# Two weight-block sums per group made by adding transfers that GpSimd issues, in a two-layer hybrid encoder trunk

## The reference, cut to what matters

```python
def swiglu(u, w_in, w_out):
    gate, up = jnp.split(u @ w_in, 2, axis=-1)
    return (jax.nn.silu(gate) * up) @ w_out

x = x + MACARON_WEIGHT * rms_norm(
    swiglu(rms_norm(x, ffn1_pre_norm[l]), ffn1_w_in[l], ffn1_w_out[l]), ffn1_post_norm[l])
```

## Time and profile before

| what | value |
|---|---|
| median of 3 runs | 2174.72 us (2173.4 to 2174.93) |
| the profiled execution's own time | 2174.53 us |
| its span in the profile | 2172.7 us |
| TensorE busy | 2141.5 us, 99% |
| VectorE busy | 1440.2 us, 66% |
| ScalarE busy | 1046.9 us, 48% |
| GpSimd busy | 75.3 us, 3% |
| mean load of the DMA engines' memory side | 101 GB/s |

### The profile page before, as it was taken

The page is one execution under the profiler, slowest core; times in us unless marked ns, Lnnn a source line. Parts: engine busy times, 40 slices in busy tenths (PEclk is TensorE's granted clock), DMA queues, the critical chain, the costliest instruction groups (busy, mean ns, idle before and its releaser), DMA issues. The chain is left out here.

```text
span 2172.7 us, 34540 instructions
## 1 busy us (share of the span) xinstructions
PE 2141.5 (99%) x14060; PEld 1926.6 (89%) x14060; DVE 1440.2 (66%) x1877; ACT 1046.9 (48%) x1802; POOL 75.3 (3%) x104
## 2 busy tenths in 40 slices
PE   8899999999999999999999999999999999999998
PEld 7899988888888899998899998887888889999987
DVE  7999735595536598873388885356944456988633
ACT  5444424655533465552375454256555436554422
POOL 0000000011000100000000000010000001000000
PEclk9999999999999999999999999999999999999999
DMA  5233332332123323323233323323322243223332
GB/s 217 91 104 108 97 97 78 127 85 79 59 78 103 140 95 110 110 86 109 85 108 117 107 88 107 97 88 117 85 69 69 78 141 117 92 107 101 105 97 78
DMA packets 80302, 218.71 MB, mean 101 GB/s; under 512 B 19216, under 2 KB 29968, under 8 KB 79376
## 3 DMA queue, kind: packets, MB, share of 16 engines
q1 hardware_dynamic: 78128, 203.92, 28.9%
q0 software_dynamic: 2016, 12.58, 1.6%
HBM read 208.87 MB, written 7.60 MB: 100 GB/s over the span
## 5 line engine op out<-in xcount | busy, mean ns | idle before, releaser
L1662 DVE TENSOR_TENSOR wlo<-raw,whi 128x1024 fp32r<-128x1024 f32 (+1 forms) x215 | 261.3, 1216 | 371.4 <-ACT whi L1137 368.7
L1137 ACT ACTIVATE whi<-raw 128x1024 fp32r<-128x1024 f32 (+1 forms) x212 | 221.1, 1043 | 422.0 <-PE ps L748 275.4
L808 PE MATMUL ps<-chi,lor 128*128 128x256 f32 x1280 | 363.0, 284 | 0.0
L670 PE MATMUL ps<-uhi,whi 128*128 128x512 f32 (+1 forms) x864 | 310.2, 359 | 4.8 <-ACT sk L1410 2.6
L672 PE MATMUL ps<-uhi,wlo 128*128 128x512 f32 (+1 forms) x864 | 302.6, 350 | 0.0
L671 PE MATMUL ps<-ulo,whi 128*128 128x512 f32 (+1 forms) x864 | 302.5, 350 | 0.0
L806 PE MATMUL ps<-chi,hir 128*128 128x256 f32 x1024 | 292.1, 285 | 6.3 <-DVE lor L1789 5.7
L807 PE MATMUL ps<-clo,hir 128*128 128x256 f32 x1024 | 290.7, 284 | 0.0
L746 PE MATMUL ps<-whi,hhi 128*128 128x512 f32 x704 | 274.5, 390 | 0.0
L747 PE MATMUL ps<-wlo,hhi 128*128 128x512 f32 x704 | 273.9, 389 | 0.0
L748 PE MATMUL ps<-whi,hlo 128*128 128x512 f32 x704 | 273.9, 389 | 0.0
(11 more groups left out here) (303 smaller groups left out, 3921.7 us busy)
## 6 DMA issues: line engine op xcount, KB each, us to landing
raw<-in_wstream_dram SPq DMA_DIRECT2D x207, 512.0 KB, 3.5
lof<-in_swstream_dram SPq DMA_DIRECT2D x80, 512.0 KB, 3.6
r<-in_swstream_dram SPq DMA_DIRECT2D x60, 512.0 KB, 4.6
ulof<-in_swstream_dram SPq DMA_DIRECT2D x20, 512.0 KB, 6.0
x_home<-x POOLq DMA_DIRECT2D x4, 1024.0 KB, 4.3
x<-x_home POOLq DMA_DIRECT2D x2, 2048.0 KB, 9.3
gain<-in_gp_dram POOLq DMA_DIRECT2D x6, 512.0 KB, 5.6
raw<-in_wstream_dram SPq DMA_DIRECT2D x10, 256.0 KB, 3.6
```

The source lines that it names most:

```text
L670: pe.matmul(o, lh, bhi, start=first, stop=False, skip_group_check=True)
L808: last = pe.matmul(o, ll, bhi, start=False, stop=True, skip_group_check=True)
L1137: act.activation(whi[:, s, 0:cols], raw[:, s % RAWS, 0:cols], ACT.Copy).then_inc(hi_done.h, 1)
L1662: dve.tensor_tensor(wlo[:, s, 0:cols], raw[:, s % RAWS, 0:cols], whi[:, s, 0:cols].bitcast(f32), ALU.subtract) \
```

## The change

The two sums `sum_3` and `sum_11` leave DVE. In their place two transfers make each sum in its slot: SP loads one block there as an ordinary transfer, and when that has landed, GpSimd issues a transfer of the other block with an addition (`accum_op=ALU.add`) into the same slot. For `sum_3` the first is W_22 (so W_22 is loaded twice, once for its own use and once for this) and the added one W_12; for `sum_11` the first is W_12 and the added one W_11 (loaded twice too). `sum_22` and `sum_4` stay on DVE. The buffer `r12` is gone, and its 4 KB become a ninth slot of the low parts; so W_11 and W_21 load behind the product nine earlier instead of eight. In the head the W_12 load of the first group moves ahead of the x tiles. GpSimd's adds for an FFN stand between its other work at the FFN's boundaries. Some waits at the end of an FFN follow the new slot numbers.

```diff
-LO_SLOTS, HI_SLOTS = 8, 5
+LO_SLOTS, HI_SLOTS = 9, 5
...
-        LO_AT, HI_AT = (136, 140, 152, 156, 148, 180, 168, 172), (56, 160, 176, 164)
+        LO_AT, HI_AT = (136, 140, 152, 156, 148, 180, 48, 168, 172), (56, 160, 176, 164)
...
-        r12 = at("r12", [P, 4, 256], 48 * kb)
...
             sp.dma_start(raw[:, 0, :], wstream[2]).then_inc(raw_ready[2].h, 16)
+            sp.dma_start(whole(0, 1, Q_C), weights(0, 0, 1, W_12)).then_inc(first11.h, 16)
             for i in range(TT):
                 sp.dma_start(x[:, i, :], xin[i]).then_inc(x_in[i].h, 16)
...
-                load_part(L, f, 1, W_12, r12[:, :, :])
+                    sp.dma_start(whole(f, 1, Q_C), weights(L, f, 1, W_12)).then_inc(first11.h, 16)
                 sp.wait_ge(gemm_done.h, gemm_done.at(L, unit))
                 load_part(L, f, 1, W_22, r22[1])
                 sp.wait_ge(split_done.h, split_done.at(L, c + 3))
                 load_part(L, f, 1, W_11, whole(f, 1, Q_A))
+                sp.wait_ge(split_done.h, split_done.at(L, c + 4))
+                sp.dma_start(whole(f, 1, Q_D), weights(L, f, 1, W_22)).then_inc(first3.h, 16)
...
-                    sp.wait_ge(*of_group(sum11, L, f, g - 1))
-                    sp.wait_ge(*of_group(sum3, L, f, g - 1))
-                    load_part(L, f, g, W_12, r12[:, :, :])
...
                     load_part(L, f, g, W_22, r22[g % 2])
+                    if g > 2:
+                        sp.wait_ge(*of_unit(unit_done, L, f, unit_no(g, Q_D) - LO_SLOTS))
+                    sp.wait_ge(*of_unit(unit_lo, L, f, unit_no(g - 1, Q_D)))
+                    sp.dma_start(whole(f, g, Q_D), weights(L, f, g, W_22)).then_inc(first3.h, 16)
                     sp.wait_ge(*of_unit(unit_done, L, f, unit_no(g, Q_A2) - LO_SLOTS))
                     load_part(L, f, g, W_21, whole(f, g, Q_A2))
+                    sp.wait_ge(*of_unit(unit_done, L, f, unit_no(g, Q_C) - LO_SLOTS))
+                    sp.dma_start(whole(f, g, Q_C), weights(L, f, g, W_12)).then_inc(first11.h, 16)
...
-                dve.tensor_tensor(whole(f, g, Q_D), r12[:, :, :], r22[g % 2], ALU.add).then_inc(sum3.h, 1)
...
-                dve.tensor_tensor(whole(f, g, Q_C), r12[:, :, :], whole(f, g, Q_A), ALU.add).then_inc(sum11.h, 1)
...
+            def add_part(L, f, g, first, to, i, signal):
+
+                pool.wait_ge(*of_landing(first, L, f, g))
+                pool.dma_start(to, weights(L, f, g, i), accum_op=ALU.add).then_inc(signal.h, 16)
+
+            def add_parts(L, f, groups):
+
+                for g in groups:
+                    add_part(L, f, g, first3, whole(f, g, Q_D), W_12, sum3)
+                    add_part(L, f, g, first11, whole(f, g, Q_C), W_11, sum11)
+
+            add_part(0, 0, 1, first11, whole(0, 1, Q_C), W_11, sum11)
             pool.wait_ge(x_in[TT - 1].h, 16)
             load_gain(0, 0)
             for t in range(TT):
                 x_power(0, 0, t)
+            add_part(0, 0, 1, first3, whole(0, 1, Q_D), W_12, sum3)
```

More of the change, by code:

```diff
@@ L388, in trunk @@
         h_lo = sem("h_lo", 2 * FT)
-        w_in = [[sem(f"w_in{i}_{a}", 16 * FINAL) for a in range(2)] for i in range(4)]
-        sum11, sum22 = sem("sum11", 2 * FINAL), sem("sum22", 2 * FINAL)
-        sum3, sum4 = sem("sum3", 2 * FINAL), sem("sum4", 2 * FINAL)
+        w_in = {i: [sem(f"w_in{i}_{a}", 16 * FINAL) for a in range(2)] for i in (W_11, W_22, W_21)}
+        first11, first3 = sem("first11", 32 * FINAL), sem("first3", 32 * FINAL)
+        sum11, sum22 = sem("sum11", 32 * FINAL), sem("sum22", 2 * FINAL)
+        sum3, sum4 = sem("sum3", 32 * FINAL), sem("sum4", 2 * FINAL)
         unit_hi, unit_lo, unit_done = sem("unit_hi", 2 * FAST), sem("unit_lo", 2 * FAST), sem("unit_done", 2 * FAST)
@@ L497, in of_tanh, with of_landing, weights @@
             return tanh_done.h, tanh_done.at(L, 2 * (f * FINAL + g - 1) + i)
+        def of_landing(signal, L, f, g):
+            return signal.h, signal.at(L, 16 * (f * FINAL + g))
+        def weights(L, f, g, i):
+            return swstream[((2 * L + f) * FINAL + g - 1) * 4 + i].rearrange("p (k c) -> p k c", c=256)
         def of_part(i, L, f, g):
@@ L1226, in unit_round @@
                 else:
-                    act.wait_ge(*of_group({Q_D: sum3, Q_B: sum22, Q_C: sum11, Q_D2: sum4}[u], L, f, g))
+                    act.wait_ge(*(of_landing if u in (Q_D, Q_C) else of_group)({Q_D: sum3, Q_B: sum22, Q_C: sum11, Q_D2: sum4}[u], L, f, g))
                 if n >= HI_SLOTS:
@@ L1736, in boundary @@
                 x_mean(L1, st, 3)
-                if st != 1:
-                    sum_11(L1, st // 2, 1)
-                    sum_3(L1, st // 2, 1)
                 u_rest(L1, st, 1)
[L1742 to L1749, removed]
-                dve.tensor_tensor(whole(f, g, Q_D), r12[:, :, :], r22[g % 2], ALU.add).then_inc(sum3.h, 1)
[L1752 to L1757, removed]
-                dve.tensor_tensor(whole(f, g, Q_C), r12[:, :, :], whole(f, g, Q_A), ALU.add).then_inc(sum11.h, 1)
             def sum_22(L, f, g):
-                dve.wait_ge(*of_group(sum11, L, f, g))
+                dve.wait_ge(*of_landing(sum11, L, f, g))
                 dve.wait_ge(*of_part(W_22, L, f, g))
@@ L1946, in ffn @@
                 unit_rest(L, f, 1, Q_C2)
-                sum_11(L, f, 2)
                 y22(L, f, 1)
@@ L1967, in ffn @@
                     unit_rest(L, f, g, Q_C2)
[L1968 to L1971, removed]
+                    if g == FINAL:
                         h_rest(L, f, 0)
@@ L2425, in _ @@
                 x_power(0, 0, t)
+            add_part(0, 0, 1, first3, whole(0, 1, Q_D), W_12, sum3)
             for L in range(DEPTH):
+                add_parts(L, 0, range(2 if L == 0 else 1, GROUPS))
                 boundary(L, 0)
@@ L2431, in _ @@
                 load_gain(L, 2)
+                add_parts(L, 1, range(1, GROUPS))
                 boundary(L, 2)
```

11 lines of the change are left out of this document (3 added, 8 removed).

## The result

| | before | after |
|---|---|---|
| time, median (range) | 2174.82 us (2173.4 to 2176.56) | 2266.43 us (2264.83 to 2271.25) |
| ratio, 95% interval | | 1.0417 (1.0404 to 1.0429) |
| span of the profiled execution | 2172.7 us | 2263.0 us |

A forecast was written before the change was run, and what follows sets the result against it. TensorE, busy 99% of the span, was taken as the bound, so relieving VectorE pays only in TensorE's waits: 2174.53 + 0 (steady) + 0.2 (head) - 1.2 (starts) = 2173.5 us, range 2167 to 2222.

The forecast's parts named there:

- the first link in the steady part: Steady groups: the W_12 load for sum_11, issued at product B's end (820.85), lands 3.4 us later, at 824.25.
- X: Time of an adding transfer from GpSimd's issue to landing: 5.3 us, ends 3.9 and 7.5.
- the slack: Steady groups: sum_22 may start as late as 829.9, so the add may take 5.5 us; 0.2 us to spare.
- 32 us for each us above 5.5: Price of slower adds: a TensorE stall in 32 groups, 8 in each of 4 FFNs; 2221 us at 7.0.
- Slow adds: Rival, chance 0.27: adds take over 5.5 us and sum_22 stalls TensorE in 32 groups; 2189 to 2221 us.
- Blocked issue: Rival, chance 0.08: GpSimd's issue of each add waits up to 1.22 us for a VectorE instruction; 2205 us.
- Relief in full: Rival, chance 0.15: early adds in the head shrink TensorE's 5.71 us idle time, low clock goes; -8.8, 2165.7 us.
- about 20.4: Length in us of a group before the change, of which VectorE is relieved of 2.3 us.
- The head: Program start: later landings use up VectorE's 4.6 us saving before group 2's D; +0.2 us, ends -1.8 to +3.1.
- the late chunk: Head: W_12 and an adding transfer ahead of the fourth weight chunk make its conversion 3.2 us later (2.6 to 3.9).
- the low part of D in group 1: Head: waits for its sum's load and add, starts at 37.8 where it was 35.28, 2.5 us late.
- The starts of the other FFNs: Three later FFN starts: TensorE's remaining waits shrink as VectorE is 2.3 us ahead; -1.2 us, ends 0 and -1.9.

The follow-up runs named there:

- experiment 1: Changed kernel with the addition taken out of GpSimd's transfers, same blocks moved as plain copies: 2175.45 us, 0.9997 of the kernel before.
- experiment 6: Changed kernel with sum_3 made by VectorE in its slot, sum_11 still an adding transfer: 2201.39 us, 1.0123 of the kernel before.
- experiment 8: Changed kernel with sum_3 and sum_11 left out, no adding transfer and no VectorE addition for them: 2168.77 us, 0.9966 of the kernel before.
- experiment 5: Changed kernel with sum_11 made by VectorE in its slot, sum_3 still an adding transfer: 2178.01 us, 1.0006 of the kernel before.

## Why the prediction was wrong

**The step that failed** is the first link in the steady part: "A load issued there lands 3.4 us later, at 824.25." That row is of a kernel in which nothing else moved at that time. The step excused the other sum with "the other sum's add was issued some 8 us earlier". In the trace it was issued 3.4 us before (840.35 and 843.77), since SP's load for it (836.60) waits for the low part of the D before it (`unit_lo`), not only for the slot. After the change, then before it:

```profile
835.31 1.22 DVE L1781 TENSOR_TENSOR lor<-lof,hir 128x1024 fp32r<-128x1024 f32 x1
```

```profile
830.10 1.22 DVE L1789 TENSOR_TENSOR lor<-lof,hir 128x1024 fp32r<-128x1024 f32 x1
```

The rows of before already give this: that low part ended at 831.3 and, with the forecast's own late `sum_22`, would end 2.5 us later. A load of 3.6 us and GpSimd's 0.3 behind it then put the add at 837.7, only 3.3 us ahead of the next end of product B at 841.0. In experiment 1, where no sum was late for TensorE, it was 3.6 us on average. So the load of W_12 ran beside an adding transfer. From its issue to that of its add it took 5.4 us on average, 1.9 more than the forecast's 3.55; with a plain transfer in the same place (experiment 1) it took 4.2, with none (experiment 6) 3.75. The load of W_21, 2.9 us ahead, is there in experiment 6 too.

**X was right within its error, the slack was not.** X was 5.6 (`sum_11`'s own 40 adds: 5.5; `sum_3`'s, beside which loads run: 6.4), forecast 5.3, with ends of 3.9 and 7.5. `sum_22` was allowed 9.1 us behind the release, or 5.5 for X. The runs put the free length at 8.8 (8.6 free, 9.1 already +0.26). Even with an undisturbed load, 3.75 + 5.55 = 9.3 is over it, and experiment 6 pays 25 us. A sum that ended 0.2 us inside its limit was not a reason for a value of 0.

**The price per us was too low at the end.** "32 us for each us above 5.5" holds for small excess. By it the true 2.2 us would be 70 us; the groups lost 87 to 89. The forecast had noted that pauses of this length might bring the low clock ("it is more") and left it out of the sum and the range.

**The rivals.** *Slow adds*, at 0.27, is what happened in its place and form: a wait for L1781 in every group. But its cause was two links, and X itself was only 5.6. (As a sign for slow adds the forecast also took the 9.3 us of the earlier trace rows, which is a transfer of four times the size.) *Blocked issue* fell: GpSimd's issue rows are 0.86 us (0.85 to 1.21). In the kernel after, 16 of the 80 adds were issued while VectorE spent over 90% of the time on instructions with two on-chip inputs; they went out 0.28 us behind the load's landing (median) and took 0.86 us each (0.87 at most). The 42 adds with under 10% of it went out 0.28 us behind as well and took 0.89 on average. *Relief in full* did not come even with plain transfers (experiment 1); its size, -8.8, was near the ceiling of -7.6 that experiment 8 shows with no second transfer at all.

**What was right.** VectorE near 1342 us (1352.9). The relief is worth nothing in the steady groups of three FFNs; in the first it is worth 0.3 us a group (20.16 in experiment 8), so VectorE's list set the length there, which the forecast's "about 20.4" hid. The head was forecast at +0.2 and came out at +2.4: the late chunk was right (3.2 against 3.6), the low part of D in group 1 was 1.2 later, and VectorE took 26.7 us from there to group 2's, not 25.7. The starts of the other FFNs, forecast at -1.2, gave nothing outside the groups: from the last product of one FFN's groups to the first of the next's the times differ from before by +0.3, -0.2 and -0.1 us.

## What to carry to other kernels

An addition moved from an engine into a transfer turns 1.2 us of busy time into latency, here 4 to 5 us of load and then 5.6 of add. So look for the first consumer and count the whole chain from the event that frees the buffer, with every other transfer that will run beside it, not with the load's duration in the kernel before. Where the sum of such a chain ends within a few tenths of its limit, forecast the side that repeats in every group; and where pauses come near 2 us, as here, add the low clock for a part of them (here 12 of 18). The sum that may go to a transfer is the one whose inputs are free a whole group ahead, as `sum_3` was (experiment 5, which lost nothing but won nothing either).

## What the runs showed of the hardware

An adding transfer of 512 KB from DRAM into on-chip memory took 5.6 us from GpSimd's issue to landing, a plain one between the same places 3.9. Its packets take nearly twice as long, 348 against 185 ns, and loads from SP that run beside it are slower too: W_12 landed 5.0 us behind its issue on average in the kernel after, 3.9 with a plain transfer beside it (experiment 1), 3.5 with none (experiment 6). GpSimd itself is busy for 0.86 us with its issue, and 0.53 with a plain one; with VectorE at work on two on-chip inputs in that time it was 0.86 as well.

The Trainium skill (DMA: Bandwidth & Descriptors, "Anatomy of one DMA — SWDGE (gpsimd) path") has a rule of about 2.0 us plus the bytes at 436 GB/s. By estimate from it a plain transfer of this size takes 3.2 us and an adding one, read as two passes, 4.4; the traces have 3.9 and 5.6, slower both times.

In the groups of the kernel after, pauses of 1.75 to 3.04 us in TensorE's work had a stretch of 3.4 us at 1.2 GHz beside them 12 times (once 6.8 us); 6 others, of 1.96 to 3.06 us, had none. In the first FFN the one of 1.90 us at 222.79 had it, the one of 2.03 at 155.74 had not. What sets the two kinds apart is not shown here.
